# Attention-projection weights moved ahead of two modulation chunks, and two output blocks computed in contraction halves

## The reference

```python
mod = (jax.nn.silu(c) @ w_ada + b_ada).reshape(B, 6, 1, D_MODEL)
sh1, sc1, g1, sh2, sc2, g2 = [mod[:, i] for i in range(6)]
h = x * (1 + sc1) + sh1
qa, ka, va, qb, kb, vb, ga, gb = jnp.split(h @ w_in, W_IN_SPLITS, axis=-1)
...
oa, ob, new_state = mixer(qa, ka, va, qb, kb, vb, pos)
merged = (jax.nn.sigmoid(ga) * (oa.reshape(B, S, DSA_OUT) @ w_pa)
          + jax.nn.sigmoid(gb) * (ob.reshape(B, S, MOBA_WIDTH) @ w_pb))
x = _layer_norm(ALPHA * x + g1 * (merged @ w_o), ln1_g, ln1_b)
h2 = x * (1 + sc2) + sh2
up, gt = jnp.split(h2 @ w_up, 2, axis=-1)
f = (jax.nn.silu(gt) * up) @ w_down
x = _layer_norm(ALPHA * x + g2 * f, ln2_g, ln2_b)
```

## Time and profile before

| | us |
|---|---|
| median of 3 runs | 591.85 (587.77 to 593.01) |
| the profiled execution, time | 586.3 |
| the profiled execution, span | 584.7 |
| TensorE busy | 531.1 (91% of the span) |
| VectorE busy | 289.7 (50%) |
| ScalarE busy | 224.2 (38%) |
| GpSimd busy | 91.0 (16%) |
| mean granted clock of TensorE in the span | 0.947 |

### The profile page before, as it was taken

How to read it: one execution, slowest core, us unless ns; L and a number is a source line. 1 busy time by engine, 2 the same in 40 slices (tenths; PEclk the granted TensorE clock), 3 DMA queues, 4 the chain that set the end, 5 groups by cost and what they waited for, 6 DMA issues and landing times.

```text
span 584.7 us, 10361 instructions
## 1 busy us (share of the span) xinstructions
PE 531.1 (91%) x4047; PEld 484.5 (83%) x4047; DVE 289.7 (50%) x560; ACT 224.2 (38%) x376; POOL 91.0 (16%) x127
## 2 busy tenths in 40 slices
PE   4767999999898999999987988999999999999990
PEld 2546999989666889798887968999999999999990
DVE  0084565456633544151477566754445455436356
ACT  1043243143323544252653445456444434232321
POOL 1001122004920000000022522720000000000005
PEclk9967899999859999899989998999999999999996
DMA  8996799995267940192362453599876674364102
GB/s 278 319 308 217 231 361 343 337 293 161 81 203 214 306 148 2 38 301 100 122 223 90 142 165 123 193 369 308 283 239 234 220 275 168 110 215 145 37 1 81
DMA packets 96719, 116.71 MB, mean 200 GB/s; under 512 B 3595, under 2 KB 87755, under 8 KB 96164
## 3 DMA queue, kind: packets, MB, share of 16 engines
q1 hardware_dynamic: 94788, 102.67, 54.0%
q0 software_dynamic: 1888, 13.44, 6.6%
HBM read 112.82 MB, written 13.57 MB: 216 GB/s over the span
## 4 chain that ended last, share of the span: by engine, by line
PE 69%; DMA 13%; DVE 6%; SPq 4%; issue 3%; ACT 3%; POOL 2%; POOLq 0%; ACTq 0%; DVEq 0%
PE psum L607 18%; PE psum L609 17%; PE psum L608 17%; DMA raw<-in_w_in 5%; DMA raw<-in_w_up 3%; PE psum L632 3%; DMA raw<-in_w_ada 3%; PE psum L802 2%; DVE w_lo L431 2%; PE psum L831 2%; PE psum L728 2%; PE psum L789 1%; PE psum L817 1%; ACT w_hi L426 1%; PE psum L906 1%
## 5 line engine op out<-in xcount | busy, mean ns | idle before, releaser
L607 PE MATMUL psum<-act_hi,w_hi 128*128 128x288 f32 x736 | 225.3, 306 | 12.2 <-DVE act_lo L1534 3.8
L431 DVE TENSOR_TENSOR w_lo<-raw,w_hi 128x1024 fp32r<-128x1024 f32 x118 | 146.3, 1242 | 171.3 <-ACT w_hi L426 171.1
L608 PE MATMUL psum<-act_lo,w_hi 128*128 128x288 f32 x736 | 220.2, 299 | 0.0
L609 PE MATMUL psum<-act_hi,w_lo 128*128 128x288 f32 x736 | 219.4, 298 | 0.0
L426 ACT ACTIVATE w_hi<-raw 128x1024 fp32r<-128x1024 f32 x118 | 124.0, 1056 | 140.4 <-PE psum L609 92.9
L607 PEld LDWEIGHTS psum<-act_hi,w_hi 128*128 128x128 f32 x736 | 141.2, 192 | 21.0 <-issue 10.9
L608 PEld LDWEIGHTS psum<-act_lo,w_hi 128*128 128x128 f32 x736 | 141.5, 192 | 0.2
L609 PEld LDWEIGHTS psum<-act_hi,w_lo 128*128 128x128 f32 x736 | 141.6, 192 | 0.0
L607 PE MATMUL psum<-f_hi,w_hi 128*128 128x288 f32 x176 | 52.4, 298 | 0.6 <-DVE f_t L1572 0.6
L608 PE MATMUL psum<-f_lo,w_hi 128*128 128x288 f32 x176 | 51.9, 295 | 0.0
L609 PE MATMUL psum<-f_hi,w_lo 128*128 128x288 f32 x176 | 51.8, 294 | 0.0
(11 more groups left out here) (180 smaller groups left out, 585.4 us busy)
## 6 DMA issues: line engine op xcount, KB each, us to landing
raw<-in_w_ada SPq DMA_DIRECT2D x24, 1024.0 KB, 7.3
raw<-in_w_up SPq DMA_DIRECT2D x22, 1024.0 KB, 6.5
raw<-in_w_in SPq DMA_DIRECT2D x19, 1024.0 KB, 5.6
raw<-in_w_down SPq DMA_DIRECT2D x10, 1024.0 KB, 5.1
out<-in_cache_kv_a POOLq DMA_DIRECT2D x16, 504.0 KB, 5.9
raw<-in_w_o SPq DMA_DIRECT2D x4, 1024.0 KB, 8.3
kvin<-in_cache_kv_a SPq DMA_DIRECT2D x8, 256.0 KB, 3.7
kvin<-in_cache_kv_b SPq DMA_DIRECT2D x16, 128.0 KB, 2.6
```

The source lines that it names most:

```text
L431: nc.vector.tensor_tensor(part(w_lo, slot4, by_rows), raw_half(rslot, hh, by_rows), part(w_hi, slot4, by_rows).bitcast(F32), ALU.subtract) ...
L607: nc.tensor.matmul(out, hi_l, hi_r, start=start, stop=False, skip_group_check=True)
L608: nc.tensor.matmul(out, hi_l, lo_r, start=False, stop=False, skip_group_check=True)
L609: return nc.tensor.matmul(out, lo_l, hi_r, start=False, stop=stop, skip_group_check=True)
```

## The change

The modulation chunks 20 and 21 are loaded behind the projection chunks instead of ahead of them: projections become n = 40, 41 and modulation 42, 43. ScalarE's and VectorE's splits of halves 40 to 43 move into the loop over the gates, at s = 12 to 15, and the four splits that stood behind the gates on each engine are gone. TensorE's order is the same up to the output blocks. There blocks 0 and 1 are computed in two passes over the contraction: tiles 0 to 3 of block 0, tiles 0 to 3 of block 1, tiles 4 to 7 of block 0, tiles 4 to 7 of block 1, with a wait for `merged_lo` at each tile.

```diff
-ADA1 = GATE0 + 8
-PAB0 = ADA1 + 2
-WO0 = PAB0 + 2
+PAB0 = GATE0 + 8
+ADA1 = PAB0 + 2
+WO0 = ADA1 + 2
...
-    if ADA1 <= n < PAB0:
+    if ADA1 <= n < WO0:
         return 20 + n - ADA1
...
-            elif n < ADA1:
+            elif n < PAB0:
                 col = 3072 + 256 * (n - GATE0)
...
-        for m in range(KT):
-            pe.wait_ge(*((gated_ready, 13 + m) if m < 2 else (z_ready, m - 1)))
-            unit_mm(pe, H_WO + m, (H_WO + m) % SPLIT, m % 2, merged_lo if m == 0 else None)
+        for k0 in (0, 4):
+            for m in range(2):
+                if k0 == 0:
+                    pe.wait_ge(gated_ready, 13 + m)
+                    pe.wait_ge(lo_ready, H_WO + m + 1)
+                slot = (H_WO + m) % SPLIT
+                wh, wl = part(w_hi, slot, False), part(w_lo, slot, False)
+                for k in range(k0, k0 + 4):
+                    pe.wait_ge(merged_lo, k + 1)
+                    mm = mm3(psum[:, m, 0:TOK], wh[:, k, :], wl[:, k, :], act_hi[:, k, :], act_lo[:, k, :], k == 0, k == KT - 1)
+                if k0 == 4:
+                    mm.then_inc(half_used, 1)
+
+        for m in range(2, KT):
+            pe.wait_ge(z_ready, m - 1)
+            unit_mm(pe, H_WO + m, (H_WO + m) % SPLIT, m % 2)
...
             nc.scalar.activation(qkvg[:, gate_slot(s), :], psum[:, s % 2, 0:TOK], ACT.Copy).then_inc(acc_free[s % 2], 1)
-            if H_GATE + s + AHEAD < H_PAB:
-                hi_static(act, H_GATE + s + AHEAD)
+            hi_static(act, H_GATE + s + AHEAD)
...
-        hi_static(act, H_PAB)
         ada_rows(20)
         oT_leading(1)
         act.wait_ge(acc_free[0], 20)
         act.wait_ge(acc_free[1], 20)
-        hi_static(act, H_PAB + 1)
-        hi_static(act, H_PAB + 2)
-        hi_static(act, H_PAB + 3)
         sigmoids(12, 16)
...
         for s in range(16):
-            if H_GATE + s + AHEAD < H_PAB:
-                lo_static(dve, H_GATE + s + AHEAD)
+            lo_static(dve, H_GATE + s + AHEAD)
...
         ada_add(20)
-        for nb in range(H_PAB, H_PAB + 4):
-            lo_static(dve, nb)
```

## The result

The changed kernel has a median of 580.79 us (578.75 to 585.77, 6 runs) against 590.59 (587.77 to 593.01, 6 runs) before; the ratio is 0.9891, with a 95% interval of 0.9852 to 0.9929. The two medians alone stand at 0.983 to each other, further apart than this ratio, so I take the gain as 1 to 2%. Before again (585.29) and the ring and splits again (580.81) are one execution each.

The account below looks back on a forecast made before the run. TensorE, busy 91% of the span, was taken as the bound, so only its idle or low-clock time counts. 1.2 + 1.5 + 2.9 + 1.6 = 7.2 us off the median 591.85 gives 584.6 us, range 580.5 to 590.5.

Parts of the forecast that it names:

- What bounds the stretch: Between gates and third output block, TensorE waits 1.4, 1.5, 1.0 and 2.2 us, with two low-clock stretches.
- Splits in the gates: Eight splits move into gates 12 to 15, covered except 0.2 us charged for the last output copy.
- Start of the projection: First projection unit no longer waits on its weights and starts at 287.75 instead of 288.95: 1.2 us saved.
- Row copy and clock: Before the second projection unit the 1.5 us row-copy wait goes; both low-clock stretches go too, 2.9 us.
- part 6: Four projection units of 3.2 us and a turn of 0.45 from 287.75 end at 301.0 instead of 307.17.
- Feeding the units: First `w_o` chunk lands after 5.5 us, at 290.6; unit 1's gated products end at 295.1, in time.
- Pause before block 0: TensorE's 1.0 us wait on the gated products before the first output block, expected to be still there.
- Halves: Block 1's first four tiles fill the 1.87 us pause inside output block 0: 1.6 us saved, at least 1.3.
- Sum: Whole changed stretch: 7.2 us saved, taking the profiled span from 584.7 to 577.5 us.
- Base: Whole kernel: the saving is taken off the median of three timed runs, 591.85 us, giving 584.6.
- Slower rival: First projection chunk lands late inside the gates; loss from a landing of 14.6 us, at longest 597.1 us; chance 0.04.

Follow-up runs that it names:

- Before again: The kernel before, run once more without an edit for its trace; one execution, 585.29 us.
- the ring and splits: The changed kernel with the old loop over the output blocks, so only the new chunk order and early splits; ratio 0.9816 to the kernel before, second execution 580.81 us.

## Why the prediction was right

- **What bounds the stretch.** Right: all four waits of the earlier trace rows changed as said.
- **Splits in the gates.** Right: they cost nothing there, since from gate 12's scores to the selection it is 19.57 us in the first trace of each kernel. The 0.2 us for the last output copy is there to the digit.
- **Start of the projection.** 1.2 us forecast, 1.27 measured (+6.45 to +5.18).
- **Row copy and clock.** 1.5 + 2.9 = 4.4 us forecast. The last unit's last matmul moved by 5.89 us, and less the start that is 4.6. The prediction has two numbers for this distance, 5.6 in its sum and 307.17 - 301.0 = 6.2 in its part 6; the measured one lies between them. The split between wait and clock rests on the two runs in which the turn was moved.
- **Feeding the units.** Right: the first `w_o` chunk landed after 5.1 us (5.5 forecast) and the second, issued behind it, after 8.8; the gated products of unit 1 were done at 296.6, which is 295.2 in the times of before, against 295.1.
- **Pause before block 0.** A small miss: 0.2 us of the gain were given back here (5.89 to 5.67), since VectorE's chain of split, `act_lo` and gated products ends 1.2 instead of 1.0 us behind TensorE.
- **Halves.** 1.6 forecast, 1.58 measured, and no wait on the residual. Against the first trace of the ring and splits, where the clock fell behind block 0's pauses, the halves are worth 3.08 us.
- **Sum.** 7.2 forecast, 7.25 in the stage. The profiled span should have been 577.5 and was 578.7, the 1.36 us ahead of the selection.
- **Base.** The median fell by 9.8 us, not 7.2, to 580.79 against a forecast of 584.6. Here the forecast was helped by luck: 580.79 lies 0.3 us above the lower end of the range, and that end is a slip, since the saving of 8 and the spread of 3 off 591.85 give 580.85. What lies ahead of the selection spreads by 14 us over the traces, enough to cover the 2.6 us, and most of it arises where both kernels run the same instructions. That speaks against a part of the change in it; no run shows it.
- **Slower rival.** Its wait was rightly worked out. Its clock was priced too low by the one trace there is: I charged one stretch of 1.5 us, and behind a chunk that came 2.9 us after ScalarE wanted it, 4.8 us went to the low clock, so that 6.8 of 7.25 us were given back. In the changed kernel ScalarE wants the chunk 6.9 us behind its last issue (257.81 to 264.71). My estimate from this trace is that the change turns into a loss at a landing near 10 us, where the prediction's own sum has 14.6 (7.4 us of slack and the saving of 7.2).

## What to carry to other kernels

Work through an ordered queue of loads and splits as one chain: taking a wait off its end is worth nothing as long as a later step of the same chain stands still, and it can cost (1.0 us in the units here, in one trace). Where a pause was followed by a low clock in your traces, add that to its price, as a risk and not as a certainty, and measure a stage from an anchor in front of it to one behind it, when whole times spread by more than the change is worth. Splitting the contraction of the first products is cheap cover for a late operand: 1.6 us for two blocks, 3.2 for three with banks of their own.

## What the runs showed of the hardware that I had not expected

- TensorE's granted clock stayed at 0.50 for 10.24 us behind pauses of 1.4 and 0.6 us in the attention part, although TensorE is shown busy for 9.96 of them, with the turn of the probabilities, the values and the sample values. Behind pauses of 1.4 to 1.6 us around unit 0 it came back after 3.41 us in all five traces.
- Whether a pause is followed by a low stretch can differ between executions of one program (D 38.39 and 36.90 us). Around block 0 the same pauses had one in two of six traces; at the projection units pauses of 1.4 us and more had one every time.
- Two 1 MB loads issued 0.5 us apart landed after 5.1 and 8.8 us, as the pair of before did (5.5 and 9.3): in both pairs the first was done while the second took nearly twice as long.
